# A sparse attention stage with its first score group, its convolution and the start of its output projection taken into earlier steps

## The reference

```python
h_n = rms_norm(h)
q, kc, vc, ks, vs, kw, vw, gl, bg, cg, hd = split(h_n @ w_in)
# _nsa: three branches, each a softmax over another set of keys
k_cmp = gelu(windows(kc, pos_k) @ ck1) @ ck2          # 15 windows of 32 tokens
v_cmp = gelu(windows(vc, pos_v) @ cv1) @ cv2
pc = masked_softmax(q @ k_cmp * 1/8);      o_c = pc @ v_cmp
ps = masked_softmax(rope(q) @ rope(ks) * 1/8); o_s = ps @ vs
pw = masked_softmax(rope(q) @ rope(kw) * 1/8); o_w = pw @ vw
yc = gate0 * o_c + gate1 * o_s + gate2 * o_w          # 512 columns
# _short_conv
yd = bg * causal_conv3(cg * hd, conv_w)               # 512 columns
h = h + concat(yc, yd) @ w_out
```

## Time and profile before

| | us |
|---|---|
| median of three runs | 2110.32 (2109.31 to 2114.49) |
| profiled execution, its own time | 2109.94 |
| its span in the trace | 2107.9 |
| PE busy | 2016.6 (96%) |
| DVE busy | 1577.1 (75%) |
| ACT busy | 1150.0 (55%) |
| POOL busy | 394.0 (19%) |
| mean granted TensorE clock | 0.989 |

### The profile page before, as it was taken

How to read it: one execution, slowest core, us unless ns; L and a number is a source line. 1 busy time by engine, 2 the same in 40 slices (tenths; PEclk the granted TensorE clock), 3 DMA queues, 4 the chain that set the end, 5 groups by cost and what they waited for, 6 DMA issues and landing times.

```text
span 2107.9 us, 31941 instructions
## 1 busy us (share of the span) xinstructions
PE 2016.6 (96%) x11820; PEld 1767.6 (84%) x11820; DVE 1577.1 (75%) x2176; ACT 1150.0 (55%) x1687; POOL 394.0 (19%) x192
## 2 busy tenths in 40 slices
PE   7999999999999999999999999999987999999997
PEld 6888987888888889888889998888975888888885
DVE  6777886677777769677778666777785588888887
ACT  5445543554454455554455535445445577777775
POOL 2222003232222310122322432223000300000000
PEclk9999999999999999999999999999998999999999
DMA  8555520455645554355544005555451588888895
GB/s 341 186 194 169 179 90 15 169 197 187 196 167 197 180 187 152 120 179 195 184 170 150 2 15 182 185 194 192 160 180 39 180 331 327 325 327 325 325 329 190
DMA packets 73395, 401.22 MB, mean 190 GB/s; under 512 B 8256, under 2 KB 8384, under 8 KB 41152
## 3 DMA queue, kind: packets, MB, share of 16 engines
q1 hardware_dynamic: 72848, 398.07, 54.1%
q10 hardware_dynamic: 432, 1.57, 0.2%
HBM read 398.57 MB, written 1.05 MB: 190 GB/s over the span
## 4 chain that ended last, share of the span: by engine, by line
PE 76%; DVE 13%; PEld 4%; ACT 3%; issue 2%; POOL 0%; DMA 0%; SPq 0%; ACTq 0%; PEldq 0%; DVEq 0%; POOLq 0%
PE psum L744 18%; PE psum L306 13%; PE psum L307 13%; PE psum L308 13%; PE psum L748 9%; DVE w_lo L290 4%; PE psum L969 2%; PE psum L957 2%; ACT w_hi L283 1%; PE psum L2803 1%; DVE w_lo L296 1%; PE psum L320 1%; PEld psum L306 1%; PEld psum L308 1%; PEld psum L307 1%
## 5 line engine op out<-in xcount | busy, mean ns | idle before, releaser
L290 DVE TENSOR_TENSOR w_lo<-ring,w_hi 128x1024 fp32r<-128x1024 f32 x498 | 742.7, 1521 | 179.4 <-ACT w_hi L283 178.0
L283 ACT ACTIVATE w_hi<-ring 128x1024 fp32r<-128x1024 f32 x744 | 739.9, 1051 | 234.2 <-PEq L500 129.1
L296 POOL TENSOR_TENSOR w_lo<-ring,w_hi 128x1024 fp32r<-128x1024 f32 x132 | 324.0, 2455 | 1079.7 <-ACT w_hi L283 1079.7
L744 PE MATMUL psum<-fT,w_hi 128*128 128x512 f32 x1760 | 422.4, 391 | 12.9 <-DVE w_lo L290 10.5
L744 PEld LDWEIGHTS psum<-fT,w_hi 128*128 128x128 f32 x1760 | 329.6, 188 | 84.3 <-issue 7.6
L306 PE MATMUL psum<-w_hi,hT_hi 128*128 128x384 f32 (+4 forms) x896 | 321.7, 359 | 12.4 <-POOL w_lo L296 4.0
L308 PE MATMUL psum<-w_hi,hT_lo 128*128 128x384 f32 (+4 forms) x896 | 310.7, 347 | 0.0
L307 PE MATMUL psum<-w_lo,hT_hi 128*128 128x384 f32 (+4 forms) x896 | 310.3, 346 | 0.0
L306 PE MATMUL psum<-w_hi,act_hi 128*128 128x512 f32 x616 | 242.4, 394 | 5.5 <-DVE act_lo L842 4.6
L307 PE MATMUL psum<-w_lo,act_hi 128*128 128x512 f32 x616 | 241.2, 392 | 0.0
L308 PE MATMUL psum<-w_hi,act_lo 128*128 128x512 f32 x616 | 239.9, 390 | 0.0
(11 more groups left out here) (485 smaller groups left out, 2413.9 us busy)
## 6 DMA issues: line engine op xcount, KB each, us to landing
ring<-in_stream SPq DMA_DIRECT2D x249, 1024.0 KB, 5.4
ring<-in_stream SPq DMA_DIRECT2D x248, 512.0 KB, 4.3
tables<-in_tables SPq DMA_DIRECT2D x1, 2261.0 KB, 19.9
gain_row<-in_gains ACTq DMA_DIRECT2D x3, 512.0 KB, 3.7
rows<-in_rows SPq DMA_DIRECT2D x1, 1288.0 KB, 22.6
X<-in_x SPq DMA_DIRECT2D x1, 1024.0 KB, 5.0
result<-X SPq DMA_DIRECT2D x2, 512.0 KB, 3.3
columns<-in_columns SPq DMA_DIRECT2D x1, 993.0 KB, 15.0
```

The source lines that it names most:

```text
L283: act.activation(part(w_hi, g, i), ring[:, k, i * PART:(i + 1) * PART], ACT.Copy) \
L290: dve.tensor_tensor(part(w_lo, g, i), ring[:, k, i * PART:(i + 1) * PART], part(w_hi, g, i).bitcast(F32), ALU.subtract) \
L296: pool.tensor_tensor(part(w_lo, g, 2), ring[:, k, 2 * PART:STEP], part(w_hi, g, 2).bitcast(F32), ALU.subtract) \
L744: pe.matmul(psum[:, 4 + 2 * (s % 2) + o, :], w[0][:, o, k, :], fT[:, k, :, :].rearrange("p a c -> p (a c)"), start=k == 0, stop=False, ski ...
```

## The change

What it does, part by part:

- Group 0 of the scores (heads 0 to 3 of the selected branch) is taken into the projection: the rotated q and k are turned after step 4, the scores of group 0 are computed after step 5, its weights on DVE in step 7, its four turns on PE after step 8. For this group alone the causal mask is added by PE, as a bf16 product of the identity with the mask in the same PSUM bank; DVE then takes only maxima out of PSUM, and ACT takes exp straight from PSUM with scale and bias.
- Groups 1 to 3 keep DVE's scaling and masking into SBUF. Their order becomes 2, 1, 3.
- The columns of hd come before those of bg. cg is scaled by the square of 1/rms, and hd is multiplied by it as it leaves PSUM, straight into n_pad; the separate product is gone. The taps and the product with bg lie between the score groups on DVE.
- k_cmp is laid out block-diagonal; the compressed scores are 8 matmuls with all 128 rows, before 16 with 64.
- o is formed transposed (`products`, `compressed`): 64 columns of v stationary, the turned unit moving. ACT and DVE write hT_hi and hT_lo from PSUM. The copy to O and its turns are gone.
- n_S lies in the parity that output step 0 does not use, so that step is split right behind the C steps; its two tiles are begun with the convolution half (`out_part`).
- DVE makes all last thirds of the C steps and of output step 0; POOL made those of two C steps and of output step 0.
- Fillers: 28 in place of 39. ACT table loads in the program: 36 in place of 35. The load of gain_row stands later.

The core of the diff:

```diff
         def proj_tensor(..., keep_last=False, begun={}):
-                for k in range(KT):
+                for k in range(KT) if (s, j) not in begun else ():
...
+                if (s, j) in begun:
+                    ins = begun[s, j]()
...
+        def masked_max_vector(dve, stage, name, units, scale, small):
+            for i, u in enumerate(units):
+                dve.wait_ge(*after(f"{u}"))
+                dve.tensor_reduce(small[:, i, :], bank(u)[:, 0:UNIT].rearrange("p (b c) -> p b c", c=P), AX.X, ALU.max).then_inc(*stage.vector())
...
+        def masked_exp_scalar(act, stage, name, units, S, scale, less, sums):
+            act.wait_ge(*after(f"{name} max"))
+            for i, u in enumerate(units):
+                for t, cols in enumerate((slice(0, P), slice(P, UNIT))):
+                    act.activation(S[:, i, cols], bank(u)[:, cols], ACT.Exp, scale=scale, bias=less[:, i, t:t + 1], accum_out=sums[:, i, t:t + 1]) \
+                       .then_inc(*stage.scalar(f"{name} exp"))
...
+        def masked_scores_tensor(pe, stage, units):
+            for label, _, _ in units:
+                b = open_bank(pe, label)
+                pe.matmul(b[:, 0:UNIT].rearrange("p (b c) -> p b c", c=P)[:, 0::2, :], ident_bf16, bias_bf16[:, 0::2, :],
+                          start=True, stop=False, skip_group_check=True)
+            for label, q, k in units:
+                pe.matmul(bank(label)[:, 0:P], q[:, 0:P], k[:, 0:P], start=False, stop=False, skip_group_check=True)
+                pe.matmul(bank(label)[:, P:UNIT], q[:, P:SEQ], k, start=False, stop=True, skip_group_check=True).then_inc(*stage.tensor(label))
...
-            n_S = take("n_S", [P, 16, UNIT])
+            out_parity = (first_step[[n for n, (kind, _) in enumerate(NETWORK) if kind == "sparse"][0]] + SPARSE_K + SPARSE_T + SPARSE_C) % 2
...
+            def products(i):
+                for u in range(4 * i, 4 * i + 4):
+                    pe.wait_ge(*after(f"used sparse pt {u}"))
+                    br, s = divmod(u, SLOTS8)
+                    c0, v = SEQ * (s // 2 % 2), (VS, VW)[br] + 64 * (s % 2)
+                    o = bank(f"sparse o {s // 4}")[slot_rows(s), c0:c0 + SEQ]
+                    pt = n_exps(i)[:, u % 4, :]
+                    pe.matmul(o, n_tok[:, 0, v:v + 64], pt[:, 0:SEQ], start=br == 0 and s % 4 < 2, stop=False, skip_group_check=True)
+                    ins = pe.matmul(o[:, P:SEQ], n_tok[:, 1, v:v + 64], pt[:, SEQ:UNIT], start=False, stop=False, skip_group_check=True)
...
-            proj_tensor(pe, "sparse", g0, N_KINDS, at, between={2: turn_plain})
+            proj_tensor(pe, "sparse", g0, N_KINDS, at, 
+                        between={2: turn_plain, 4: turn_rotated, 5: lambda: scores(0), 8: lambda: turn_units(0)})
...
-                        keep_warm(pe, b, 0 if which else 11)
...
+            scores(3)
+            turn_units(2, 4)
+            turn_units(1, 4)
+            for b in range(2):
+                open_bank(pe, f"sparse o {b}")
+            keep_warm(pe, bank("sparse o 0"), 8)
+            products(0)
+            products(2)
...
+            turn_units(3)
+            products(1)
+            compressed(0).then_inc(*sparse.tensor("sparse o 0"))
+            compressed(1)
+            products(3).then_inc(*sparse.tensor("sparse o 1"))
...
-            turn_tensor(pe, "sparse", sparse, 4, [f"used sparse o {t}" for t in range(TT)])
-            pe.wait_ge(*after("sparse conv"))
-            out_tensor(pe, "sparse", at, 4, warm=16)
+            for t in range(TT):
+                open_bank(pe, f"sparse out 0 {t}")
+                wait_split(pe, g)
+                pe.wait_ge(*after("sparse conv"))
+                out_part(t, range(4, KT), first=True)
...
+            out_tensor(pe, "sparse", at, 4, begun={(0, t): lambda t=t: rest(t) for t in range(TT)})
...
+            proj_copies_scalar(act, "sparse", at, N_KINDS, n_place, {2: plain}, ahead=True,
+                               later={4: gate, 5: rotated, 6: lambda: exps(0)})
...
-            pool.wait_ge(lo_last_ready, first_step[at] + len(N_KINDS) + 1)
-            proj_pool(pool, first_step[at] + len(N_KINDS), SPARSE_C)
+            pool.wait_ge(lo_last_ready, first_step[at] + len(N_KINDS) + SPARSE_C + 1)
...
-            does(None, dve.tensor_tensor, n_pad[:, :, 2:2 + SEQ], n_cg[:, :, :], n_hd[:, :, :], ALU.mult)
...
+                               later={3: lambda: (squared_row(), rotate(0)), 4: lambda: rotate(1), 5: windows, 7: lambda: weights(0)},
+                               between={5: lambda: largest(0)})
...
-            yield from column_steps([kc, vc, w[:, 1304:]], SPARSE_T)
+            yield from column_steps([kc, vc, w[:, 1816:], w[:, 1304:1816]], SPARSE_T)
```

More of the change, by code:

```diff
@@ L1748, in sparse_tensor @@
-            scores(range(8, 16))
-            def turn_units(i):
-                for u in range(4 * i, 4 * i + 4):
-                    turn_unit_tensor(pe, sparse, f"sparse pt {u}", n_S[:, u, :], f"sparse p {i}", {8: 12}.get(u, 0))
-            for i in range(4):
-                turn_units(i)
+            for t in range(TT):
+                for j in range(4):
+                    c0 = (4 * t + j) * 2 * CMP_PAD
+                    ins = pe.matmul(b[:, c0:c0 + 2 * CMP_PAD], n_qn[:, j, t * P:(t + 1) * P], n_kcmp.rearrange("p i n -> p (i n)"), start=True, stop=True)
@@ new lines, in sparse_tensor, with out_part @@
+            products(3).then_inc(*sparse.tensor("sparse o 1"))
+            g = g0 + len(N_KINDS) + SPARSE_C
+            w = [x[:, g % 2, :].rearrange("p (k c) -> p k c", k=KT) for x in (w_hi, w_lo)]
+            def out_part(t, ks, first=False, last=False):
+                for k in ks:
+                    ins = three_passes(pe, bank(f"sparse out 0 {t}")[:, 0:COLS], [x[:, k, t * P:(t + 1) * P] for x in (hT_hi, hT_lo)],
+                                       [x[:, k, 0:COLS] for x in w], first and k == ks[0], last and k == ks[-1])
+                return ins
@@ new lines, in rotated, with exps @@
+            def rotated():
+                for t in range(TT):
+                    act.wait_ge(*after(f"sparse qr {t}"))
+                    does(f"used sparse qr {t}", n_qr[:, :, t * P:(t + 1) * P], four(bank(f"sparse qr {t}")), ACT.Copy)
+                    act.wait_ge(*after(f"sparse kt {t}"))
+                    does(f"used sparse kt {t}", n_kt[:, :, t * P:(t + 1) * P],
+                         bank(f"sparse kt {t}")[:, 0:2 * P].rearrange("p (i c) -> p i c", i=2), ACT.Copy)
+            def exps(i):
+                mine = slice(4 * i, 4 * i + 4)
+                if i > 0:
+                    softmax_scalar(act, sparse, f"sparse {i}", n_exps(i), n_max[:, mine, :], n_sum[:, mine, :])
+                    return
+                masked_exp_scalar(act, sparse, f"sparse {i}", N_GROUPS[i], n_exps(i), 64 ** -0.5, n_max[:, mine, :], n_sum[:, mine, :])
@@ new lines, in turned_units, with output, hidden @@
+            def turned_units(i):
+                for u in range(4 * i, 4 * i + 4):
+                    act.wait_ge(*after(f"sparse pt {u}"))
+                    does(f"used sparse pt {u}", n_exps(i)[:, u % 4, :], bank(f"sparse pt {u}")[:, 0:UNIT], ACT.Copy)
+            def output(b):
+                act.wait_ge(*after(f"sparse o {b}"))
+                does(f"sparse hi {b}", hT_hi[:, 2 * b:2 * b + 2, :], bank(f"sparse o {b}").rearrange("p (c t) -> p c t", c=2), ACT.Copy)
+            def hidden(which):
@@ L1800, in sparse_scalar @@
+            hidden(0)
+            split_hi(act, c0 + SPARSE_C, c0 + SPARSE_C)
+            hidden(1)
+            act.activation(warm[:, :], eps, ACT.Exp)
             for which in range(2):
```

312 lines of the change are left out of this document (183 added, 129 removed).

## The result

| | before | changed |
|---|---|---|
| median | 2109.99 us (2109.31 to 2114.49, 4 runs) | 2086.45 us (2084.61 to 2088.18, 4 runs) |
| profiled execution, its own time | 2109.94 | 2084.61 |
| its span | 2107.9 | 2082.8 |

The changed kernel takes 0.9884 of the time of the kernel before, 95% interval 0.9867 to 0.9901: 23.5 us less by the medians, 25.3 less by the two profiled executions. I had forecast 2090.6 in a range of 2084 to 2098. The direction and most of the size are as forecast; the gain is 4 to 6 us larger than my sum.

The account below looks back on a forecast made before the run. PE was taken to pace the front, then a DVE chain and a PE chain the back. Front -2.5, two legs -19.05 and clock +2.2 make -19.35 us from 2109.94, so 2090.6, range 2084 to 2098.

Parts of the forecast that it names:

- front: First projection matmul to last window matmul, paced by PE: 8.75 us removed, 5.05 added, 1.2 left over, so -2.5.
- DVE leg: From PE's last window matmul to the end of group 1's weights, paced by DVE: 26.0 us.
- PE leg: From group 1's turns to the first output projection matmul, paced by PE: 17.05 us at full speed.
- clock: PE's clock low after waiting beside the DVE leg, slowing the start of the PE leg: +2.2 us.
- unit of products: In the PE leg, 256 + 128 moving columns with 64 stationary: 0.65 us each, 10.4 for 16.
- rival B: Units of products overlap as score units do: 16 times 0.2 us less, 3.3, so 2087.3; chance 0.15.
- The 11 fillers: PE fillers in the front, from 1552.56 to 1554.74: removing them was to save 2.18 us.
- POOL's third: PE's wait in the front for the late last third of a split made by POOL: removing it saves 1.07 us.
- Rival C: Clock stays low into the products, half the PE leg at half speed: 8.5 us for 2.2, 2096.9; chance 0.12.
- Rival A: DVE late in the front, its group 0 maxima and weights fully on the path: 4.6 us, 2095.2; chance 0.15.
- Rivals D and E: D: low clock through the output projection too, 2122, chance 0.03. E: earlier start lost at next wait, 2109, chance 0.02.
- The table loads: Two ACT loads in step 4, 1.28 and 1.30 us by the trace; the skill's 2.66 each would add 0.6.

Follow-up runs that it names:

- e1: Changed kernel with products reordered so neighbours mostly write the same column half; first projection matmul to first output projection matmul 130.5 us, against 127.4.
- e8: Kernel before with only the early rstd_row copy and no fillers before the first C step; first projection to first output projection matmul 148.0 us, against 152.1.
- e6: Changed kernel with group 0 taken back behind the C steps, ahead of group 2; first projection to first output projection matmul 131.3 us, against 127.4.
- e4: Changed kernel with the last thirds of C steps 2 and 3 back on POOL; first projection to first output projection matmul 128.1 us, against 127.4.
- e3: Changed kernel with more fillers in the DVE leg's waits (12, 8, 20 for 4, 4, 4); first projection to first output projection matmul 125.4 us, against 127.4.
- e7: Changed kernel with the output projection's first half waiting for all of o; router's first matmul 146.0 us behind the first projection matmul, against 144.6.
- e2: Changed kernel without its 28 fillers in the sparse layer; first projection matmul to first output projection matmul 125.5 us, against 127.4.

## Why the prediction was right, and where it was off

| step | forecast | measured |
|---|---|---|
| front (first matmul to last window matmul) | -2.5 | 90.3 to 87.5, -2.8 |
| wait left before the first C step | 1.2 | 1.34 |
| DVE leg | 26.0 | 25.3 |
| PE leg at full clock, without the clock's term | 17.05 | 12.6 |
| clock | +2.2 | +2.0 |
| output projection and after | 0 | as before |

*The two-part reading was right.* DVE's chain and then PE's, one behind the other, is what the windows show, and the last wait of PE is for group 1's weights, where the order of the program put it. The lag behind the last window matmul was 1.3 us and not 1.9, because I had left out the 0.45 us in front of the third C step; the rest of the DVE leg came out by its rows.

*The step that was off is the price of a unit of products*, 0.65 forecast and 0.345 measured. The 16 units took 5.8 us and not 10.4, and these 4.6 are most of the 5.3 us by which the two legs together beat my sum (the other 0.7 is in the DVE leg). I had the lower bound, 0.445 from the score units, and rival B named the mechanism (e1 shows it), but I took the row without overlap as the nearest, and even my lower bound was too high: two half-width products side by side cost what one costs alone. So what happened is rival B, to which I had given 0.15, and more strongly than it said. That the measured time lies within the range all the same is owed to the other terms, and to a range of 14 us.

*The front came out right with errors in it that cancel.* The 11 fillers were priced as 2.18 us of removable work. But without them and with nothing in their place 1.4 us are lost in the first C step, to the clock (e8). In the changed kernel the turns of group 0 take over that part. I priced them as filling 1.4 us of a wait; e6 shows that without them another 1.5 us is lost to the clock. POOL's third was priced too high: I had PE start at 1564.2, but PE was at the second C step until 1564.3, and 0.45 us in front of each C step are there without POOL as well. So of the 1.07 only about 0.6 could be had, which is what e4 gave back. In turn a wait costs about 0.2 us more than its length: over the one of 2.94 us the starts of two neighbouring matmuls lie 3.22 us apart, and 0.11 in dense work.

*The clock's term was right in size,* +1.25 in group 1's turns and +0.75 in the 8 fillers (against the 1.36 and 1.82 us that they take in e3), 2.0 in all. Rival C (half of the PE leg slow) did not come: the products from 1596.1 on ran at 1.00. The Trainium skill ("TensorE: Matmul & The Clock Gate", HAM oscillation) has bursts that start cold after each longer wait, and the trace agrees for the turns behind the 4.16 us wait; it stops there because dense work follows.

*Rival A* (DVE late in the front) did not come: no wait over 2 us for w_lo in steps 5 to 8, and the 1.34 before the windows is what was left in the sum. *Rivals D and E* did not come: the output projection ran at 1.00 and nothing behind the stage was longer.

*The table loads.* Both went behind the split of step 5, took 1.28 and were followed by the next ACTIVATE 1.29 and 1.30 us after their start (1514.22 to 1515.51, 1515.77 to 1517.07). ACT still waited 3.65 us afterwards. The drain of 1.38 us that the Trainium skill has behind each load ("ScalarE: Activation LUTs", What ACT_TABLE_LOAD costs) is not seen here, and it was right to go by the row.

What stays open: whether the 0.4 us that the spans gain beyond the stage is more than scatter. And parts of the back were not tried one by one: the taps between the groups, the block-diagonal k_cmp, the missing turns of O and the early split of output step 0. What they gave is in the sums of the two legs by their rows, and no run takes one of them back alone, except for the cover that the early split makes possible (e7).

## What to carry to other kernels

Split a stage where the engine in the lead changes, and sum each leg by its own engine: that gave both terms here within 1 us wherever the trace had a row for the operation. Before you price a form the trace lacks, ask which part of the array its neighbours leave free; the order in which halves alternate is worth a factor of two. A filler is worth something only inside a wait, and what fills a wait (work or filler) can be worth its length plus what the clock would cost behind it (1.4 and 1.5 us here); a filler behind the last wait is work on the path.

## What the runs showed of the hardware

- Two float32 products with 64 stationary columns in opposite halves of the columns run side by side: 0.345 us per unit of 384 columns, against 0.65 to 0.70 in the same half. The overlap is complete, where score units on alternating halves of the rows took 0.445.
- A PE wait of 2.94 us after dense work left the granted clock at 1.00 in the 4 us behind it. Waits of 2.66 and 2.65 us before the windows in e6 and e8, after dense work too, were followed by 0.68 and 0.66 over 4 us: the clock was still 1.00 when the work began and fell 1.3 to 1.4 us into it. Behind the wait of 5.51 us it was 0.50 from the start and 0.70 over 9.4 us. The wait's length alone does not tell; what decides was not tried and stays open.
- Behind the wait ahead of group 1's turns the clock came back with fillers (0.71 over the 8 fillers, 1.00 behind them) and with products alone (e2: 0.50 in the turns, 1.00 from 1596.3 on).
- The four instructions of DVE's first tap, 1.14 us alone, take 3.25 beside a POOL subtraction, and a two-piece split 4.56 in place of 2.36 (e4).
